# A mixture-of-experts layer whose expert jobs change from 128 to 96 token slots, on an 18-slot weight ring, with the down projections of two chunks run as one

## The reference, cut to what matters

```python
logits = (h @ router_w + router_b)
top_v, top_i = lax.top_k(logits, TOP_K)          # 4 of 32 experts
gates = jax.nn.softmax(top_v, axis=-1)
def expert_block(args):
    xblk, e = args
    act = clamped_swiglu(xblk @ w_gate_up[e] + b_gate_up[e])
    return act @ w_down[e] + b_down[e]
out = ...add(yb * slot_gate[:, None])            # back to the tokens, weighted
```

## Time and profile before

| | us |
|---|---|
| median of 3 runs | 1364.05 (1364.03 to 1365.1) |
| the profiled execution, its own time | 1361.84 |
| its span, first to last instruction | 1360.1 |
| PE busy | 1181.8 (87% of the span) |
| gate matmuls (L634), 5120 instructions | 602.9 |
| down matmuls (L667), 5120 instructions | 289.0 |
| expert weights | 384 loads of 1 MB |
| mean granted TensorE clock | 0.938 of full speed |

### The profile page before, as it was taken

One profiled execution on the slowest core, in us unless ns is written; L12 is line 12 of the kernel. 1 busy time (PEld: TensorE's weight loads), 2 busy tenths in 40 slices (PEclk: granted clock), 3 DMA queues, 4 the chain that ended last, 5 costly groups with the idle time before them and its releaser, 6 DMA issues.

```text
span 1360.1 us, 32747 instructions
## 1 busy us (share of the span) xinstructions
PE 1181.8 (87%) x11932; PEld 513.8 (38%) x11933; DVE 502.6 (37%) x1386; ACT 178.3 (13%) x328; POOL 245.2 (18%) x250
## 2 busy tenths in 40 slices
PE   6999998976999989999999997889998898878770
PEld 3674554551343333333333343223333233322220
DVE  2002332243453334444443353333443343433337
ACT  3013332210010101111111100001110010000002
POOL 0503433001112111111111111111112111111110
PEclk9999999986999999999999999889999899988885
DMA  9511210043899999999999999999999999999957
GB/s 378 225 62 63 77 67 12 32 155 142 361 420 419 420 419 419 419 419 418 408 389 399 419 420 420 420 418 419 420 421 418 420 419 421 420 420 420 420 232 308
DMA packets 71453, 454.87 MB, mean 334 GB/s; under 512 B 11013, under 2 KB 11325, under 8 KB 19974
## 3 DMA queue, kind: packets, MB, share of 16 engines
q1 hardware_dynamic: 61374, 430.49, 77.1%
q0 software_dynamic: 9360, 22.08, 4.3%
q10 hardware_dynamic: 696, 1.98, 0.5%
HBM read 444.37 MB, written 14.71 MB: 338 GB/s over the span
## 4 chain that ended last, share of the span: by engine, by line
PE 67%; DMA 25%; DVE 3%; issue 3%; ACT 1%; SPq 0%; DVEq 0%; POOLq 0%
PE bank L634 31%; PE bank L667 16%; DMA arena<-in_w_down 13%; DMA arena<-in_w_gate_up 11%; PE bank L424 8%; PE bank L494 4%; PE bank L440 3%; PE bank L453 1%; DVE xs L1275 1%; PE bank L481 1%; PE bank L467 1%; PE bank L619 1%; PE bank L398 1%; PE bank L573 1%; DMA xs<-in_x 0%
## 5 line engine op out<-in xcount | busy, mean ns | idle before, releaser
L634 PE MATMUL bank<-arena,hT 128*32 128x512 f32 x5120 | 602.9, 629 | 39.8 <-DMA arena<-in_w_gate_up 31.1
L634 PEld LDWEIGHTS bank<-arena,hT 128*32 128x32 f32 x5120 | 172.6, 115 | 443.9 <-issue 384.6
L667 PE MATMUL bank<-arena,hT 128*32 128x256 f32 x5120 | 289.0, 382 | 18.2 <-DMA arena<-in_w_down 18.1
L667 PEld LDWEIGHTS bank<-arena,hT 128*32 128x32 f32 x5120 | 167.4, 111 | 147.7 <-DMA arena<-in_w_down 27.2
L941 POOL DMA_INDIRECT y_rows<-hT,arena x80 | 80.4, 1005 | 655.3 <-DVE hT L1217 647.9
L1201 DVE TENSOR_TENSOR arena<-bank,gain 128x512 f32<-128x512 f32 x80 | 55.3, 692 | 347.9 <-PE bank L634 347.9
L828 ACT ACT_TABLE_LOAD x48 | 61.6, 1283 | 498.0 <-issue 497.7
L920 POOL DMA_INDIRECT hT<-h_rows,arena x83 | 84.6, 1019 | 201.1 <-issue 195.6
L424 PE MATMUL bank<-hT,arena 128*128 128x512 f32 x224 | 103.6, 610 | 0.8 <-ACT hT L726 0.8
L828 ACT ACTIVATE arena<-arena 128x256 f32<-128x256 f32 x80 | 33.3, 417 | 407.6 <-DVE arena L1203 407.6
L905 POOL TENSOR_SCALAR arena<-arena,st 128x128 f32<-128x128 f32 (+3 forms) x48 | 51.4, 1082 | 116.6 <-DVE st L1012 116.5
(11 more groups left out here) (138 smaller groups left out, 620.0 us busy)
## 6 DMA issues: line engine op xcount, KB each, us to landing
arena<-in_w_gate_up SPq DMA_DIRECT2D x256, 1024.0 KB, 20.9
arena<-in_w_down SPq DMA_DIRECT2D x128, 1024.0 KB, 22.0
arena<-in_w_in SPq DMA_DIRECT2D x10, 1024.0 KB, 18.1
arena<-y_rows SPq DMA_DIRECT2D x8, 1024.0 KB, 12.0
arena<-in_w_out SPq DMA_DIRECT2D x4, 1024.0 KB, 21.6
arena<-bias_by_dist POOLq DMA_DIRECT2D x6, 512.0 KB, 3.9
xs<-in_x SPq DMA_DIRECT2D x4, 512.0 KB, 6.9
h_rows<-arena POOLq DMA_DIRECT2D x4, 512.0 KB, 2.9
```

Of the source, the lines that this page charges most:

```text
L634: mm = pe.matmul(bank[c][j * CH:(j + 1) * CH, :].rearrange("p (g n) -> p g n", g=2), xT[:, c, k * CH:(k + 1) * CH], w[:, :, j * Q:(j + 1) ...
L667: mm = pe.matmul(bank[c][j * CH:(j + 1) * CH, 0:Q], aT[:, c, k * CH:(k + 1) * CH], w[:, j * Q:(j + 1) * Q], start=(k == 0), stop=(k == KT ...
```

## The change

Five things change together.

1. A job has at most 96 token slots (`JT`, 3 chunks) in place of 128, so an expert with more than 96 tokens gets a second job. The number of jobs is rounded up to an even one, and TensorE's and SP's loops take two jobs ("halves") in one loop body.
2. The ring has 18 slots in use: units 0 to 5 of odd jobs lie in slots 12 to 17. SP may load units 0 to 5 of job n as soon as job n-2 has read them; units 6 to 11 still wait for job n-1. Units 0 to 5 of job 1 are loaded before the router has finished.
3. TensorE runs the indices of the next job after the first half of the gates, not ahead of them. The conditions on the number of chunks now stand inside the loop over k.
4. The downs of chunks 0 and 1 are one: 64 stationary tokens, 512 columns, two column groups, results in one bank. Chunk 2, where there is one, is done ahead of them in the old form. The pair starts when both chunks' activations are there, and its pass frees the slots.
5. Chunks 0 and 1 are scattered by one indirect DMA of 2 KB rows; the third chunk's scatter is always issued, with rows that are skipped when there is none, and both wait for the pair's result. The bias of the pair is spread over 512 columns.

The diff, cut to its core:

```diff
-NCH = P // CH
+NCH = 3
+JT = NCH * CH
+HALF = 6
...
             def wait_read(job, u, low=None):
...
+            def ring_slot(half, u):
+                return u + JOB_UNITS if half and u < HALF else u
...
+            for n in range(HALF):
+                if n == HALF - 2:
+                    sp.wait_ge(ssq_done, 2 * TT)
+                    sp.wait_ge(tr_done, 4 * TT)
+                    for b in range(2):
+                        sp.wait_ge(h2_out[b], 16 * TT // 2)
+                sp.wait_ge(unit_full[n], 16)
+                load_unit(1, n, 1)
+            sp.wait_ge(jobs_done, 2)
...
+            load_part(1, 1, 1, range(HALF, JOB_UNITS), counted(1), 0)
+            with sp.Fori(0, more) as pair:
+                for half in range(2):
+                    job = pair * 2 + (2 + half)
...
+                    load_part(e, job, half, range(HALF), low, pair * 2 + half)
+                    load_part(e, job, half, range(HALF, JOB_UNITS), low, pair * 2 + (1 + half))
...
+                def down_pair(k):
+                    w = unit(KT + k // 2)[:, (k % 2) * D:(k % 2 + 1) * D]
+                    for g in range(2):
+                        mm = pe.matmul(bank[3][g * 2 * CH:(g + 1) * 2 * CH, :],
+                                       aT_pair[:, k].rearrange("p c s -> p (c s)"), w[:, g * 2 * Q:(g + 1) * 2 * Q],
+                                       start=(k == 0), stop=(k == KT - 1), tile_position=(0, g * 2 * CH))
...
-                indices(job + 1)
-                pe.wait_ge(x_done, job + 1)
...
+                pe.wait_ge(x_done, job + 1)
+                for k in range(KT // 2):
+                    pe.wait_ge(unit_full[k], full)
+                    with pe.If(chunks > 2):
+                        gate_step(2, k)
+                    gate_step(1, k)
+                    gate_step(0, k)
+                indices(job + 1)
                 with pe.If(chunks > 2):
                     gate_rest(2)
                 gate_rest(1)
                 gate_rest(0)
+                pe.wait_ge(y_done, job + 1)
                 with pe.If(chunks > 2):
+                    pe.wait_ge(act_done, low + (AHEAD - 2))
+                    for k in range(KT):
+                        if k % 2 == 0:
+                            pe.wait_ge(unit_full[KT + k // 2], full)
+                        down_third(k)
+                pe.wait_ge(act_done, low + AHEAD)
+                for k in range(KT):
+                    if k % 2 == 0:
+                        pe.wait_ge(unit_full[KT + k // 2], full)
+                    down_pair(k)
...
+            with pe.Fori(0, pairs) as pair:
+                for half in range(2):
...
+                pool.wait_ge(y_done, job + 2)
+                pool.indirect_dma_start(y_rows, ...idx_s[:, 0:1]..., yb_third, ...)
+                pool.indirect_dma_start(y_halves, ...idx_s[:, 1:2]..., yb_pair, ...)
...
-                dve.stream_shuffle(bt, bias_row[:, :], [0] * CH).then_inc(bias_spread, 1)
+                dve.stream_shuffle(bt_third, bias_row[:, 4 * Q:5 * Q], [0] * CH)
+                dve.stream_shuffle(bt, bias_row[:, 0:4 * Q], [0] * CH).then_inc(bias_spread, 1)
...
+                dve.tensor_tensor(yb_pair, bank[3][:, :], bt[:, 2 * Q:4 * Q], ALU.add).then_inc(y_done, 1)
```

More of the change, by code:

```diff
@@ L84 @@
 C_AFTER = 473
-C_END = C_AFTER + 49
+C_BEFORE = C_AFTER + 56
+C_LIMITS = C_BEFORE + 56
+C_EVEN = C_LIMITS + 5
+C_SKIPG = C_EVEN + 32
+C_END = C_SKIPG + 1
 ROWS = 5
@@ L616, in indices @@
                 pe.wait_ge(hot_done, job + 1)
-                for c in range(NCH):
+                for c in range(LISTS):
                     for t in range(TT):
@@ L626, in _, with run_job, unit @@
             pe.wait_ge(jobs_done, 2)
-            def run_job(job, chunks, before_job, low):
+            def run_job(job, half, chunks, low):
+                full = job * 16 + 16
+                def unit(u):
+                    return ring[:, u + JOB_UNITS if half and u < HALF else u, :]
                 def gate_step(c, k):
-                    w = ring[:, k, :].rearrange("p (g n) -> p g n", g=2)
+                    w = unit(k).rearrange("p (g n) -> p g n", g=2)
                     for j in range(4):
@@ L703, in _ @@
+            with pe.Fori(0, pairs) as pair:
+                for half in range(2):
+                    job = pair * 2 + half
+                    run_job(job, half,
+                            pe.value_load(jobs_i[0:1, 2, bass.ds(job, 1)], min_val=LEAST, max_val=NCH),
+                            pe.value_load(jobs_i[0:1, 3, bass.ds(job + 1, 1)], min_val=4, max_val=COUNT_MAX))
         @block.scalar
@@ L833, in _ @@
                 with act.If(chunks > 2):
-                    with act.If(chunks > 3):
-                        sigmoid(3)
                     sigmoid(2)
@@ L948, in _ @@
                 with pool.If(next_chunks > 2):
-                    with pool.If(next_chunks > 3):
-                        gather(3, gathered)
                     gather(2, gathered)
@@ L1226, in _ @@
                 with dve.If(chunks > 2):
-                    with dve.If(chunks > 3):
-                        swiglu(3)
                     swiglu(2)
```

239 lines of the change are left out of this document (107 added, 132 removed).

## The result

Eleven executions of the changed kernel have a median of 1364.49 us (1362.01 to 1366.93), eleven of the kernel before, on the same chips, 1362.6 (1360.87 to 1365.36). The ratio is 1.0021, 95% interval [1.0011, 1.0031]: **slower by about 0.2%**, 2 to 3 us, where 3.3 us faster was forecast. The time lies in the forecast range, the sign is the wrong one. The profiled execution took 1366.48 us (span 1364.7), and the profiled one of before 1361.84; these two differ by 4.6 us, where the ratio stands for 2 to 3, so sizes from this pair are good to some 2 us.

What follows compares the result with a forecast made beforehand. Weight stream as bound: restart 341.8 + 961.5, ramp about 2, lull 5.1 gives 1310.4; tail 5.6 gives 1316.0, 5.1 under 1321.15; scatters +1.8 leave -3.3, so 1364.05 becomes 1360.7 us; range 1354 to 1378.

Steps and rivals of the forecast that it cites:

- Jobs, start, restart: Loop's beginning: 32 jobs, first gates at 318.7 us, 2.5 us earlier; weight loads resume at 341.8, early loads cancelling to -1.5 us.
- 366 units x 2.627: Weight stream after its restart: 366 units at the old kernel's 2.627 us each, 961.5 us, reaching 1303.3.
- the restart: SP's in-order queue: the next load, unit 6 of job 1, waits for job 0's gates and goes out at 341.8 us.
- other parts: Gathers, scatters and SP's loads beside the stream: gathers cost 0, scatters off the path except at the end, loads hidden.
- The lull: Slow stretch of the stream at 640 to 748 us: its 5.1 us loss is given back whole.
- TensorE's jobs: Matmul time in the loop: 33.1 us for three chunks, 27.6 for two, 971 us in all, 23.5 short of the stream's end.
- The issue term: Between TensorE's jobs: some 1.2 us of issue a job, for 1.37 before.
- The waits for DMA: TensorE's waits for weights over the loop: down from 49 to some 20 us.
- The tail: After the last landing: last matmul 5.6 us behind with a slow stretch, 4.5 before; then 1.8 us more for the scatters.
- B: Rival, 26%: conditions and register reads in the gate loop make TensorE the bound; 1376 us at 1.2 us more a job.
- C: Rival, 5%: the pair's two column groups do not overlap, 6.9 us more a job, +197 us, 1558.
- D: Rival, 9%: no change, since the start is not earlier and slow last pair and scatters take most of the gain; 1363 us.

Runs made afterwards that it cites:

- order: Changed kernel with units 0 to 5 of job n+1 loaded ahead of units 6 to 11 of job n: 0.9971 of the kernel before, 1359.53 us.
- nopref: Changed kernel with six units of job 1 loaded after the job table, not before it: 1.0011 of the kernel before.
- before_bias5_timed: Kernel before with bias rows of five quarters for three, the added two loaded but not read: 1.0033 of the kernel before.
- after_bias3: Changed kernel with bias rows of three quarters for five, right biases left out, for timing alone: 0.9971 of the kernel before, 1357.76 us.
- after_shift: Changed kernel, complete, with bias rows of three quarters, the pair's biases built on VectorE by eight copies: 0.9959 of the kernel before, 1359.67 us.
- split: Changed kernel with downs of chunks 0 and 1 apart again, on four groups of 256 columns, old adds and scatters: 1.0267 of the kernel before, 1401.28 us.

## Why the prediction was wrong

- **Jobs, start, restart: right.** There were 32 jobs. The first gates came at 318.15 (forecast 318.7) in the profiled execution, and between 314.35 and 318.39 in those of the other kernels with the early start, so a part of this hit is luck. Eight loads stand in one issue group up to 342.4, and the stream runs from 341 (forecast 341.8). The early loads and the late restart cancel, as order and nopref show from both sides.
- **The stream, "366 units x 2.627": wrong, the step that failed.** The 2.627 us a unit was taken over from the kernel before, and the diff's line `5 * Q` for `3 * Q` was given no cost, neither at "the restart" nor at "other parts". By measure that line costs 0.3% in the kernel before (before_bias5_timed) and 0.5 to 0.6% in the changed one (after_bias3, after_shift), 4.5 to 8 us. From the first gates to the last job's unit 7 the forecast has 981.2 us; the changed kernel took 988.3 and 987.8, with short rows 982.3 and 983.1, and with these it is 0.4% faster than before (after_shift, 0.9959), more than the forecast 3.3 us.
- **The lull: right, with too small a cause.** It was given back whole (5.1 us), and it went. TensorE's jobs of three chunks became 1.3 us shorter, where 0.3 was forecast.
- **TensorE's jobs: right in kind.** The stop ahead of the pair is 3.0 us (forecast 3.2), the pair 7.09 (6.9), the half clock after the stop as foreseen, two chunks 26.3 (27.6), three 32.1 (33.1). The issue term of 1.2 us a job was the error: it is zero. Ahead of the jump now stand 32 instructions of some 220 ns (7.09 / 32), where 64 of 55 ns (7.09 / 128) stood. The 13 us that two more switches of the array's layout in each job were said to add did not come: between gates, indices and pair no idle time is seen (594.16 follows 587.15 + 7.09, 572.53 and 573.01 follow their predecessors as closely). The 0.16 and 0.26 us that the prediction read as such a drain are put down to issue in its rows.
- **The waits for DMA: wrong.** About 20 us were forecast, 48.6 came. They are what the shorter jobs and the slower stream leave.
- **The tail: undersized.** From unit 7 to the last matmul it took 17.6 us, 3.3 more than before, where +1.1 was forecast. The gates behind unit 7 were put at full clock, 4.4 us, and took 5.8 (6.1 before); the stop and the slow pair came as forecast. The scatters were +1.4 (forecast 1.8).
- **The rivals.** B, that conditions in the k loop make TensorE the bound, is false: the earlier trace rows and the timelines after show no gap at a condition, and two-chunk jobs are longer by the stop alone, less the issue gap that went (26.3 for 24.6; both have one slow stretch). A stall at a jump of the loop is real, though: split shows one, of 7.1 us in the mean. C, no overlap of two groups, is false (7.09 us). D, no change because the start isn't earlier, has the wrong cause. The outcome, slower by 0.2% through the rate of the stream, was no rival at all, and that the time lies in the range is owed to the width that B and C gave it.

## What to carry to other kernels

When a stream of weights is the bound, price every other transfer by what it does to the stream and not by its bytes: the 8 KB more in four rows to four partitions cost here seven to twelve times their share, and VectorE could build the same values in time that it had to spare. A prefetch is worth only what the in-order queue behind it allows; look at the first load that must wait, not at the first that may go. With two jobs in one body, look at the packets of the instruction queue: with the old form of the downs such a body was 2.7% slower than the kernel before. And compare profiled executions from a point inside them, such as the first gates, not from their start.

## What the runs showed of the hardware

- A load of four rows of 5120 bytes beside a saturated stream goes with some 16 slow packets of 8192 bytes (over 345 ns) in the microsecond behind it, 347 ns in the mean for 316 beside rows of 3072 bytes. The rows in two transfers gave 0.15 to 0.2%, in 20 packets of 1024 bytes to 20 partitions 0.3%, 8 KB fewer bytes 0.6%.
- The gap at the loop's jump is 1.37 us behind a chunk of 64 short down instructions and nothing behind the pair. In the run that moved 133 packets of code for 14 it is 6.3 to 8.0 us at 13 of 15 jumps.
- A stop of 3.0 us is followed, in most two-chunk jobs but not in all, by a stretch in which 32 instructions take 8.78 us for 7.09. The granted clock there was 0.66, so for part of it the lower of TensorE's two clocks (1.2 GHz for 2.4) was given.
- A switch from two column groups to four (594.16 follows 587.15 + 7.09) and from full width to four (573.01 follows 572.53 + 0.55) shows no idle time.
